# A throwaway square root behind the last gelu, and decode's window values loaded in three pieces

## The reference

```python
    kwin = jnp.concatenate([kwb, kw], axis=1)
    vwin = jnp.concatenate([vwb, vw], axis=1)
    ...
    o_w = jnp.einsum('bqgrk,bkgd->bqgrd', _masked_softmax(s_w, m_w).astype(dt), vwin)
```

```python
    y = xf * lax.rsqrt(jnp.mean(xf * xf, axis=-1, keepdims=True) + RMS_EPS) * g.astype(jnp.float32)
```

## Time and profile before

| | |
|---|---|
| median of three runs | 2016.91 us (2016.57 to 2017.2) |
| the profiled execution's own time | 2016.73 us |
| its span in the trace | 2014.9 us |
| PE busy | 1529.5 us, 76% |
| DVE busy | 1286.9 us, 64% |
| POOL busy | 700.4 us, 35% |
| ACT busy | 296.4 us, 15% |
| bytes read from DRAM | 661.00 MB |

### The profile page before, as it was taken

One profiled execution on the slowest core, in us unless ns is written; L12 is line 12 of the kernel. 1 busy time (PEld: TensorE's weight loads), 2 busy tenths in 40 slices (PEclk: granted clock), 3 DMA queues, 4 the chain that ended last, 5 costly groups with the idle time before them and its releaser, 6 DMA issues.

```text
span 2014.9 us, 22586 instructions
## 1 busy us (share of the span) xinstructions
PE 1529.5 (76%) x7549; PEld 679.8 (34%) x7549; DVE 1286.9 (64%) x3101; ACT 296.4 (15%) x733; POOL 700.4 (35%) x843
## 2 busy tenths in 40 slices
PE   6999889999997888986777856666556666666666
PEld 5446675637683454541333411110001111111111
DVE  5988627523576878645578985459896445454445
ACT  3000135421131222102111101000000000000001
POOL 5952103400373233333332333333333333333332
PEclk9999886999997899996788966665666666566665
DMA  5323434364789999999999999999999999999997
GB/s 192 107 69 99 138 101 133 103 259 158 229 286 415 412 408 416 398 413 419 413 400 417 422 386 414 421 414 419 402 409 417 413 413 421 416 415 409 417 413 290
DMA packets 142631, 669.64 MB, mean 332 GB/s; under 512 B 17268, under 2 KB 51764, under 8 KB 72564
## 3 DMA queue, kind: packets, MB, share of 16 engines
q0 software_dynamic: 74880, 545.29, 66.0%
q1 hardware_dynamic: 67636, 122.90, 17.8%
HBM read 661.00 MB, written 19.65 MB: 338 GB/s over the span
## 4 chain that ended last, share of the span: by engine, by line
DMA 32%; PE 17%; DVE 10%; issue 8%; POOL 3%; ACT 0%; DVEq 0%; POOLq 0%
DMA ex_uv<-in_peer_uv,idxT 20%; DMA w_out<-in_peer_uv,idxT 12%; PE ex_acc L2398 9%; PE ex_hb L2292 3%; DVE ex_uv L2566 2%; POOL ex_uv L2183 2%; POOL w_out L2183 1%; DVE w_out L2566 1%; PE ex_late L2317 1%; DVE ch_iu L1633 1%; PE ex_late L2365 1%; DVE ch_ci L1633 1%; DVE ch_v L1630 1%; PE ex_late L2332 1%; DVE ch_sc L1630 1%
## 5 line engine op out<-in xcount | busy, mean ns | idle before, releaser
L2292 PE MATMUL ex_hb<-ffn_gain,spread 24*128 24x512 bf16 x1040 | 339.6, 480 | 409.4 <-DVE ex_uv L2566 265.6
L2566 DVE SCALAR_TENSOR_TENSOR ex_uv<-ex_uv,ex_hb 128x1024 f32<-128x1024 f32 x344 | 416.0, 1219 | 310.7 <-DMA ex_uv<-in_peer_uv,idxT 265.6
L2183 POOL DMA_INDIRECT ex_uv<-in_peer_uv,idxT x344 | 325.4, 946 | 602.6 <-PE ex_acc L2398 517.4
L2566 DVE SCALAR_TENSOR_TENSOR w_out<-w_out,ex_hb 128x1024 f32<-128x1024 f32 x176 | 213.2, 1219 | 156.3 <-DMA w_out<-in_peer_uv,idxT 126.5
L2292 PEld LDWEIGHTS ex_hb<-ffn_gain,spread 24*128 24x128 bf16 x1040 | 53.3, 98 | 732.3 <-DVE ex_uv L2566 391.5
L2398 PE MATMUL ex_acc<-ex_uv,wts 128*32 128x512 f32 x1376 | 276.5, 947 | 0.0
L2183 POOL DMA_INDIRECT w_out<-in_peer_uv,idxT x172 | 163.7, 952 | 301.1 <-PE ex_acc L2398 261.7
L2717 ACT ACTIVATE ex_gelu<-ex_dots 128x4 f32<-128x4 f32 (+1 forms) x131 | 26.9, 205 | 957.5 <-DVE ex_uv L2566 637.8
L2398 PE MATMUL ex_acc<-w_out,wts 128*32 128x512 f32 x704 | 143.1, 948 | 0.0
L2398 PEld LDWEIGHTS ex_acc<-ex_uv,wts 128*32 128x32 f32 x1376 | 47.8, 147 | 160.5 <-issue 160.5
L799 POOL TENSOR_TENSOR at_prob<-at_prob,at_coef 128x256 f32<-128x256 f32 (+3 forms) x32 | 40.1, 1253 | 119.8 <-DVE at_coef L909 119.7
(11 more groups left out here) (527 smaller groups left out, 2192.4 us busy)
## 6 DMA issues: line engine op xcount, KB each, us to landing
sgT<-in_late_w SPq DMA_DIRECT2D x24, 1024.0 KB, 7.5
w_q<-in_peer_w_q SPq DMA_DIRECT2D x15, 1024.0 KB, 6.0
gate_ring<-in_w_in SPq DMA_DIRECT2D x6, 2048.0 KB, 9.2
ex_uv<-in_peer_uv,idxT POOLq DMA_INDIRECT x344
ks_rows<-in_ks_pages SPq DMA_DIRECT2D x64, 64.0 KB, 2.2
vs_rows<-in_cache_v_sel SPq DMA_DIRECT2D x64, 64.0 KB, 2.1
vc<-in_vc_pages SPq DMA_DIRECT2D x64, 64.0 KB, 2.1
gate_ring<-in_kc_pages SPq DMA_DIRECT2D x64, 64.0 KB, 2.1
```

Source lines behind the costliest of these rows:

```text
L2183: pool.indirect_dma_start(slot(s).rearrange("p j n -> p (j n)"), None, table, bass.IndirectOffsetOnAxis(ap=S.idxT[:, t:t + 1], axis=0))\
L2292: last = pe.matmul(hb[s % 2][:, CHUNK * h:CHUNK * h + CHUNK], spread[p, k % LOAD, :], h_rows[p, l % 2, CHUNK * h:CHUNK * h + CHUNK], start ...
L2566: dve.scalar_tensor_tensor(out=rows_, in0=rows_, scalar=1.0, in1=hb[s % 2][:], op0=ALU.mult, op1=ALU.mult, accum_out=dots[:, B % 2, c:c + ...
```

## The change

ScalarE gets one more instruction: behind the last gelu of the last batch a Sqrt of one column of `ss` goes to another column of `ss` that nobody reads. In decode SP no longer loads all of `vwin` and then patches it. It issues three DMAs to disjoint parts, one behind the other, all on `v_in`: the new rows into partition 0, row 0 of each sequence; rows 1 to 3 of partition 0 from the cache (8 runs of 1536 bytes); and partitions 1 to 127 from the cache. The weights of the merge come behind them, SP's wait is gone, and so is the semaphore `v_new`. TensorE waits for all three (`v_in` at 48).

```diff
             sp.wait_ge(E["hid_done"], 2)
-            sp.dma_start(vwin.rearrange("p b w n -> p b (w n)"),
-                         io["cache_v_win"].rearrange("a b (p w) g d -> p (a b) (w g d)", w=WT)).then_inc(E["v_in"], 16)
+            old = io["cache_v_win"].rearrange("a b (p w) g d -> p (a b) w (g d)", w=WT)
+            sp.dma_start(vwin[0:1, :, 0, :], new_rows.rearrange("(a b) n -> a b n", a=1)).then_inc(E["v_in"], 16)
+            sp.dma_start(vwin[0:1, :, 1:, :], old[0:1, :, 1:, :]).then_inc(E["v_in"], 16)
+            sp.dma_start(vwin[1:].rearrange("p b w n -> p b (w n)"),
+                         old[1:].rearrange("p b w n -> p b (w n)")).then_inc(E["v_in"], 16)
             load_merge(sp, io, S, merge_half(S, 0), 0)
-            sp.wait_ge(E["v_in"], 16)
-            sp.dma_start(vwin[0:1, :, 0, :], new_rows.rearrange("(a b) n -> a b n", a=1)).then_inc(E["v_new"], 16)
...
-            pe.wait_ge(E["v_new"], 16)
+            pe.wait_ge(E["v_in"], 16 * 3)
             pe.wait_ge(E["pw_kept"], 1)
...
                     act.activation(gelu[:, B % 2, c0:c1], dots[:, B % 2, c0:c1],
                                    ACT.Gelu_apprx_tanh).then_inc(E["gelu_done"], 1)
+                if B == END:
+                    act.activation(ss[:, TILES + 2:TILES + 3], ss[:, TILES:TILES + 1], ACT.Sqrt)
                 late_work(B - 1, 1)
```

More of the change, by code:

```diff
@@ L1235, in stage_decode @@
         pb = ps("dpb", [P, 512])
-        names = ("consts", "zeroed", "kw_in", "q_turned", "rows_saved", "gates_in", "v_in", "v_new", "q_ready", "qz_ready",
+        names = ("consts", "zeroed", "kw_in", "q_turned", "rows_saved", "gates_in", "v_in", "q_ready", "qz_ready",
                  "kw_ready", "hid_done", "parts_kept", "hid_summed", "gh_ready", "w2_done", "ck_kept", "cv_kept", "sc_done",
```

## The result

The changed kernel takes 2090.27 us (median of 4 runs, 2087.81 to 2091.69) against 2016.89 us, a ratio of 1.0363 with a 95% interval of 1.0345 to 1.0381: 73.4 us slower. The profiled execution took 2090.89 us, its span is 2089.2 us. In the experiments the kernel before was timed anew beside each group of versions, so its median differs a little there (2017.06, 2018.05 or 2017.69 us).

The account below looks back on a forecast made before the run. The experts stage's gathers and TensorE were taken to bound the span, with the change in serial decode and the end. From 2016.7 us, +72.8 for the one-engine load and -1.0 for the square root gave 2088.5 us, range 2074 to 2110.

Parts of the forecast that it names:

- The big load on one engine: Decode: the 127-row load runs on one DMA engine, as 127 is prime; TensorE starts 72.8 us later; 83%.
- The size of it: Decode's big load: 1016 packets at 84.4 ns, 85.8 us, plus 2.4 us, landing at 514.2 us.
- the other estimate: Decode's big load at the skill page's 27 GiB/s an engine: 72 us instead of 86, sum about 2075.
- what is moved behind it: Merge weights issued behind the big load land by 524.7 us, before the merge stage at 528.9: hidden, 4 us to spare.
- The total: Whole kernel: 2016.7 us plus 72.8 less 1.0 gives 2088.5 us, +3.6%.
- The place where SP is held: Decode: with the queue full, SP is held inside the third load, perhaps until 505 us.
- The square root: Kernel's end: Sqrt table loaded beforehand starts the last root earlier, -1.0 us; Square needs no other table.
- The cover: Behind the last gelu: the throwaway root is hidden before the first Square, with 1.2 us of cover left.
- The wait that goes: Decode: with all three loads in time, TensorE starts L1489 at some 440.2 instead of 441.45 us, -1.2 us.
- that gain would hold: Decode: the 1.2 us survives at L1496, since four matmuls of 1.92 us in all stand in front of it.
- the spread load: Rival in decode: the big load spreads over 16 or 8 engines, both gains stay, 2014.5 us; 11%.
- the slow single engine: Rival in decode: one engine at 123 ns a packet, 2128 us; 5%, with whatever else lies above 2110.

Follow-up runs that it names:

- quiet: Changed kernel without the throwaway square root, SP waiting for all three loads before issuing the merge weights: 2090.54 us, ratio 1.035.
- sqrt_only: Kernel before plus the throwaway square root alone, loads as before: 2014.17 us against 2017.06, ratio 0.999.
- split_112_sqrt: Changed kernel, square root included, with partitions 1 to 127 in two loads of 112 and 15 rows: 2011.93 us against 2017.06, ratio 0.9977.
- three_tables: Kernel before plus three throwaways (Sqrt, gelu, Sqrt) behind the last gelu: 2016.04 us against 2017.69, ratio 0.9992.
- cuts on 16 engines: Changed kernel with partitions 1 to 127 as 112 and 15 rows: from 16, 2014.16 us (with square root 2011.93); from 1, without it, 2014.55.
- cut at 16: Changed kernel with partitions 1 to 127 loaded as 16 to 127 and 1 to 15: 2014.16 us without the square root, 2011.93 with it.

## Why the prediction was right

- **The big load on one engine**, with its shape read off the small packets: right. One engine at 25 GB/s for 60 us on end, one closing packet in `quiet`, and the count of rows as the cause by five cuts (112 twice, 122, 124, and 127 from partition 0), whose small packets, where they could be counted, are as many as the divisor says.
- **The size of it**: a packet was put at 84.4 ns and took 83.4 (24.6 GB/s), so the other estimate, 72 us for the load, was too low: 1016 packets are 84.7 us. Issue to start was put at 88.2 us and took 92.8. The term that was mis-sized stands under "what is moved behind it": I asked whether the merge weights would land late for the merge stage (they don't) and not whether they would slow the load ahead of them. That is 5.8 us, less 1.2 that the load itself was under its estimate.
- **The total** of 2088.5 us came nearer to the measured 2090.27 than its terms deserve, and by luck. In the profiled execution decode grew by 77.6 us, not 72.8, and the stages ahead of it happened to take 4 us less.
- **The place where SP is held**: foreseen inside the third weight load until about 505 us, it was the first, until 500.1. That SP stands there for 77.66 us cost nothing.
- **The square root**: -1.0 us between the second Square and the root, right in all traces with a throwaway Sqrt (1.02 us from one to the other in the changed kernel, `sqrt_only` and `split_112_sqrt`, 1.00 in `three_tables`); the times alone don't show it. Square keeps the Sqrt table. The cover was put at 1.2 us and was 0.6 in the changed kernel, whose last matmuls ran at full clock.
- **The wait that goes** ("that gain would hold"): wrong, though it didn't matter for the forecast. The cuts on 16 engines show the earlier start of 1.2 us, and a stage of 63.7 to 65.0 us where the old one took 63.9 to 64.3. With the cut at 16 the four matmuls that were to stand in front of L1496 took 1.05 us at full clock and not 1.92, so TensorE waited there.
- **The rivals**: the spread load is out by the share of 6.5%, one engine's, and the slow single engine (123 ns a packet) by the rate of 83.4 ns.

## What to carry to other kernels

Before a load is cut to spare a wait, count the rows of the piece that is left: 127, 122 or 124 rows out of 128 turned a load that landed after 10 us into one that TensorE waited for until 93, 50 and 37 us behind its issue, while 112 and 15 rows cost nothing. In a DMA view of loads whose own runs are of 512 bytes or more, the packets under 512 bytes, divided by the number of loads that ended in it, were the engines that each ran on (12 for 24 rows, 16 and 15 for 112 and 15, one for 127). A wait that is removed ahead of TensorE is worth what the next one, and the clock, leave of it. And the cover for a throwaway is to be read where TensorE has its full clock: at half it looks larger than it will be.

## What I had not expected of the hardware

- Four engines alone were slower each (115 ns for a packet of 2 KB) than one, two or all sixteen (83.4, 83.1 and 84.4 ns).
- Loads issued behind an unfinished load on few engines delayed it by 4.8 to 5.8 us, even where fifteen other engines had been idle: by the estimate above its packets took 140 ns in that stretch instead of 83.4.
- The time that TensorE's last four matmuls leave for the throwaway is shorter at the full clock: 2.32 us from the last gelu to the first Square at a granted clock of 1.00, 3.20 at 0.50.
